# Experts' weights streamed in pairs of panels, 16 KB per partition in one row

## The chip, the cores and the metric

One core of a Trainium2 chip runs the whole program. The metric is the device time of one execution in microseconds, as the median of the runs; smaller is better.

## What is computed

Three transformer blocks follow each other on 256 tokens of width 1024, all in f32. The change touches only the experts' layer of the second block: every token picks 4 of 32 experts, and each expert is a two-layer network of its own.

```python
N_EXPERTS = 32; TOP_K = 4; D_FF_EXPERT = D_MODEL   # 1024
logits = xt @ router_w + router_b
top_logit, top_idx = lax.top_k(logits, TOP_K)
top_gate = jax.nn.softmax(top_logit, axis=-1)
...
# for every expert e, on the tokens that picked it:
#   hidden = x_e @ w1[e] + b1[e]        w1[e]: 1024 x 2048, 8 MB
#   glu, lin = the two halves of hidden, clipped to 7
#   act = glu * sigmoid(1.702 * glu) * (lin + 1)
#   y_e = act @ w2[e] + b2[e]           w2[e]: 1024 x 1024, 4 MB
# the output sums gate * y_e over the four experts of a token
```

## The kernel before

The first and the third block and the second block's mixers read their weights through `core.ring`, six places (`RING`) of 8 KB per partition (`SLOT`, 2048 f32), 1 MB each. The experts' layer takes those six places over and adds a tensor of its own, `expert_ring`, which has eleven more.

An expert's weights are twelve panels of 1 MB. Panels 0 to 7 are rows of `w1`: the array `w1` is laid out so that panel j is 128 rows of 8 KB, one for each partition. Panels 8 to 11 are `w2`, two blocks of 128 rows of 4 KB each, which go side by side into a place. Of the 17 places, twelve hold one panel number each; the other five are second places for panels 0 to 4 (`TWICE`), used by experts of odd number, so that these panels of the next expert can be on their way while the present ones are still in use.

The work goes in units, a unit being one expert with at most 64 of its tokens. Here there are 32 units. TensorE does, in this order for each unit u: the bias (L2733), panels 0 to 7 (L2738, eight matmul instructions a panel), the scatter of the unit before (L2514), the gather of the next unit's tokens (L2486), turns of gates, hidden values and tokens (L2747, L2752, L2492), a bias (L2757), and panels 8 to 11 (L2768). Ahead of each panel it waits for that panel's own semaphore (`panel(j)`), and behind each it counts up `used`. VectorE and ScalarE do the activation (L2797 to L2803, L2780) in the time of scatter and gather.

SyncE (SP) issues all loads, in an order that is written out: the function `load` waits until `used` tells that the place is free and issues one transfer of 1 MB. Up to `AHEAD` (units 0 to 17) panels 0 to 4 of unit u+1 are issued ahead of panels 5 to 11 of unit u; from there on, behind them. Unit 0 and the second places are filled by `load_first`, during the end of the mixers (L2862, L2864). When the last unit is done, its scatter and the residual add follow, the block ends, and the third block's first loads are issued (L246).

Of the kernel before, what the change touches and what calls it, by code (L numbers as in the profile page):

```python
# [6 lines left out]
F32 = mybir.dt.float32  # L7
# [7 lines left out]
P = 128  # L15
TOK = 256
NB = TOK // P
D = 1024
# [4 lines left out]
RING = 6  # L23
SLOT = KG * PANEL
# [13 lines left out]
N_EXPERTS, TOP_K = 32, 4  # L38
# [101 lines left out]
class Signal:  # L140


    def __init__(self, sem):
        self.sem, self.base, self.raised = sem, 0, 0
# [2283 lines left out]
def mixture_of_experts(core, h, norm, bias, ring, rw):  # L2428
# [6 lines left out]
    with ExitStack() as s:  # L2435
# [14 lines left out]
        used = ring.used  # L2450
# [7 lines left out]
        def pair_count(eng):  # L2458
            return eng.value_load(unit_int[0:1, MAX_UNITS:MAX_UNITS + 1], min_val=E // 2, max_val=MAX_UNITS // 2)
# [43 lines left out]
        def scatter(pe, u):  # L2503

            pe.wait_ge(copied.sem, copied.at(u))
            pe.wait_ge(gates_copied.sem, gates_copied.at(u))

            pe.wait_ge(added.sem, added.at(u * 4))  # L2510
            for t in range(4):
                for i, (rows, _) in enumerate(halves):

                    mm = pe.matmul(ps[:, 2 + 2 * i + t // 2, t % 2 * TOK:t % 2 * TOK + TOK], ytok[rows, t * P:t * P + P],  # L2514
                                   selt[rows, :], start=True, stop=True)
                    if t % 2 == 1:
                        mm.then_inc(scattered.sem, 1)
# [8 lines left out]
        with ExitStack() as s2:  # L2526
# [14 lines left out]
            with core.block() as block:  # L2541
                @block.gpsimd
                def _(pool):
                    pool.memset(acc[:, :, :], 0.0)

                    pool.memset(ytok[:, :], 0.0)
                    pool.memset(selt[:, :], 0.0).then_inc(cleared.sem, 1)
# [138 lines left out]
        with core.block() as block:  # L2686
            @block.sync
            def _(sp):
                def load(u, turn, panels, odd, e):
                    for j in panels:  # L2690

                        sp.wait_ge(used.sem, turn * PANELS + (j + 1))
                        sp.dma_start(ring.panel(j, odd), ring.weights(e, j)).then_inc(ring.loaded_at(j, odd).sem, 16)

                def expert(u):
                    return sp.value_load(unit_int[0:1, bass.ds(u, 1)], min_val=0, max_val=E - 1)
                twice, once = range(TWICE), range(TWICE, PANELS)

                with sp.Fori(1, AHEAD) as v:
                    load(v * 2, v * 2 - 2, twice, 0, v * 2)  # L2700
                    load(v * 2 - 1, v * 2 - 2, once, 1, v * 2 - 1)
                    load(v * 2 + 1, v * 2 - 1, twice, 1, v * 2 + 1)
                    load(v * 2, v * 2 - 1, once, 0, v * 2)

                def in_turn(v, before, even, odd):
                    load(v * 2 - 1, v * 2 - 2, once, 1, before)
                    load(v * 2, v * 2 - 2, twice, 0, even)
                    load(v * 2, v * 2 - 1, once, 0, even)
                    load(v * 2 + 1, v * 2 - 1, twice, 1, odd)
                with sp.Fori(AHEAD, E // 2 - 1) as v:  # L2710
                    in_turn(v, v * 2 - 1, v * 2, v * 2 + 1)
                n = pair_count(sp)
                with sp.Fori(E // 2 - 1, n) as v:
                    in_turn(v, expert(v * 2 - 1), expert(v * 2), expert(v * 2 + 1))
                last = sp.value_load(unit_int[0:1, MAX_UNITS + 1:MAX_UNITS + 2], min_val=E // 2 - 1, max_val=MAX_UNITS // 2 - 1)
                load(last * 2 + 1, last * 2, once, 1, expert(last * 2 + 1))

            @block.tensor
            def _(pe):
                n = pair_count(pe)  # L2720
                with pe.Fori(0, n) as v:
                    for odd in range(2):
                        u = v * 2 + odd
                        def panel(j):
                            sig = ring.loaded_at(j, odd)
                            pe.wait_ge(sig.sem, sig.at((v if j < TWICE else u) * 16 + 16))
                            return ring.flat(j, odd)
                        pe.wait_ge(expert_picked.sem, expert_picked.at(u + 1))
                        pe.wait_ge(xg_ready.sem, xg_ready.at(u + 1))

# [31 lines left out]
                        for q in range(4):  # L2762
                            w = panel(8 + q)
                            for i in range(2):
                                k = 2 * q + i
# [53 lines left out]
                                             in1=core.x[:, k, :], op0=ALU.mult, op1=ALU.add)  # L2819


PANELS, TWICE, AHEAD = 12, 5, 9


class ExpertRing:


    def __init__(self, core, s):
        self.core = core
        self.more = s.enter_context(core.nc.sbuf_tensor("expert_ring", [P, PANELS - RING + TWICE, SLOT], F32))  # L2830
        self.loaded = [core.counter(f"expert_panel{j}") for j in range(PANELS + TWICE)]
        self.used = core.counter("expert_panel_used")

    def slot(self, j, odd):

        return PANELS + j if odd and j < TWICE else j

    def loaded_at(self, j, odd):
        return self.loaded[self.slot(j, odd)]

    def flat(self, j, odd=0):
        n = self.slot(j, odd)
        return self.core.ring[:, n, :] if n < RING else self.more[:, n - RING, :]

    def panel(self, j, odd=0):
        return self.flat(j, odd) if j < 8 else self.flat(j, odd).rearrange("p (k n) -> p k n", n=D)

    def weights(self, e, j):

        if j < 8:  # L2850
            return self.core.a["w1"][bass.ds(e * 8 + j, 1)].rearrange("a p n -> p (a n)")
        return self.core.a["w2"][bass.ds(e * 4 + (j - 8), 1)].rearrange("a (k p) n -> p (a k) n", p=P)

    def load_first(self, sp):

        core = self.core
        total = len(core.stream)
        for j in [*range(RING, PANELS), *range(RING)]:
            if j < RING:

                sp.wait_ge(core.panel_used.sem, core.panel_used.at(range(j, total, RING)[-1] + 1))
            sp.dma_start(self.panel(j), self.weights(0, j)).then_inc(self.loaded[j].sem, 16)  # L2862
        for j in range(TWICE):
            sp.dma_start(self.panel(j, 1), self.weights(1, j)).then_inc(self.loaded_at(j, 1).sem, 16)  # L2864


def moe_layer(core, h, bias, ring, rw):
# [491 lines left out]
def tokens_last(x):  # L3359

    return np.ascontiguousarray(x.reshape(x.shape[0], -1, P).transpose(2, 1, 0))
# [35 lines left out]
def layout(i):  # L3397
    f = {k: np.asarray(v) for k, v in i.items()}
    a = {"x": tokens_last(f["x"][0]), "p": np.stack([tokens_last(f["p"][l, 0]) for l in range(DEPTH)])}
# [6 lines left out]
    for l in range(DEPTH):  # L3406
        g, u = f["w_ffn_gate"][l].reshape(D, FF_T, P), f["w_ffn_up"][l].reshape(D, FF_T, P)
# [34 lines left out]
    a["lora"] = np.ascontiguousarray(np.concatenate([  # L3442
        np.concatenate([f["decay_up_2"][0], f["iclr_up_2"][0]], axis=0), f["gate_up_2"][0]], axis=1))
    a["router"] = np.ascontiguousarray(f["router_w_2"][0].reshape(DT, P, N_EXPERTS).transpose(1, 0, 2))
    a["w1"] = f["exp_w1_2"][0].reshape(N_EXPERTS * 8, P, SLOT)
    a["w2"] = f["exp_w2_2"][0].reshape(N_EXPERTS * 4, 2 * P, D)
    a["eb"] = np.ascontiguousarray(np.concatenate([f["exp_b1_2"][0], f["exp_b2_2"][0]], axis=1))

    w = f["w_in_3"][0]
# [29 lines left out]
```

## Time and profile before

| | us |
|---|---|
| median of 3 runs | 2482.25 |
| lowest, highest | 2480.29, 4030.77 |
| the profiled execution's own time | 2479.19 |
| its span, first to last instruction | 2477.4 |
| TensorE busy | 2321.4 (94%) |
| DMA, bytes moved | 619.06 MB, mean 250 GB/s |

The profiled execution is 3.06 us below the median, and 1.8 us of its own time lie outside the span. The span is cut into 40 slices of about 62 us in the page's rows of digits; the experts' layer is the long stretch from slice 21 to slice 36. The mean over the span hides that the core's DMA engines are busy to a quite different degree in that stretch than elsewhere.

### The profile page before, as it was taken

The page shows a single profiled execution, that of the slowest core. Times are in us where ns is not written, and L with a number is a line of the kernel's source. Part 1 is how long each engine was busy: PE and PEld are TensorE (multiplying, and loading weights), DVE is VectorE, ACT ScalarE, POOL GpSimd, SP SyncE. Part 2 cuts the span into 40 slices and gives each one's busy share as a digit, 9 for nine tenths or more (in the row PEclk, how much of TensorE's full clock was granted, in tenths as well). Part 3 has the DMA queues.
Part 4 walks back from the last instruction along what each step waited for, and adds up shares of the span by engine and source line. Part 5 has one row for each costly group of instructions (what it writes and reads, how often), then busy time and mean ns, then how long its engine had stood idle before and what let it go on. Part 6 is the DMA issues. An engine that isn't in the chain of part 4 may idle for free. (4 is left out here: it accounts for less than half of the span.)

```text
span 2477.4 us, 31797 instructions
## 1 busy us (share of the span) xinstructions
PE 2321.4 (94%) x12991; PEld 1532.0 (62%) x12991; DVE 660.2 (27%) x1448; ACT 395.8 (16%) x824; POOL 71.1 (3%) x80
## 2 busy tenths in 40 slices
PE   8999999999899999998789999999999999979998
PEld 7778788877688877876633333333333333348786
DVE  3142100024300022626223222222222222242222
ACT  2210110014200012224201000000110000012331
POOL 0110010000000000011000000000000000000000
PEclk9999999999999999999889999999999999989999
DMA  6334644455754454310669999999999999952422
GB/s 262 119 104 145 214 153 144 159 195 190 296 188 153 140 190 139 134 36 2 283 265 417 417 418 417 417 417 418 416 417 417 418 417 417 417 225 94 162 71 91
DMA packets 105020, 619.06 MB, mean 250 GB/s; under 512 B 9856, under 2 KB 11136, under 8 KB 48128
## 3 DMA queue, kind: packets, MB, share of 16 engines
q1 hardware_dynamic: 103216, 611.10, 63.3%
q10 hardware_dynamic: 1712, 6.63, 0.8%
q8 instruction: 71, 1.16, 0.2%
q14 instruction: 21, 0.17, 0.0%
HBM read 616.63 MB, written 1.05 MB: 249 GB/s over the span
## 5 line engine op out<-in xcount | busy, mean ns | idle before, releaser
L391 PE MATMUL ps<-x_res,ring 128*128 128x256 f32 x2560 | 568.6, 383 | 21.3 <-ACT x_res L953 12.9
L391 PEld LDWEIGHTS ps<-x_res,ring 128*128 128x128 f32 x2560 | 488.5, 192 | 97.5 <-issue 22.4
L2738 PE MATMUL ps<-expert_ring,moe_xg 128*64 128x512 f32 x1152 | 262.4, 596 | 24.4 <-DMA expert_ring<-w_dram 24.3
L391 PE MATMUL ps<-first_arena,ring 128*128 128x256 f32 x1088 | 239.4, 379 | 1.4 <-DMA ring<-w_o_dram 1.4
L2768 PE MATMUL ps<-expert_ring,mix_y 128*64 128x512 f32 x1024 | 226.8, 595 | 0.0
L391 PEld LDWEIGHTS ps<-first_arena,ring 128*128 128x128 f32 x1088 | 206.6, 190 | 29.8 <-DMA ring<-w_o_dram 1.8
L2738 PE MATMUL ps<-ring,moe_xg 128*64 128x512 f32 x896 | 202.8, 598 | 15.8 <-DMA ring<-w_dram 15.2
L2738 PEld LDWEIGHTS ps<-expert_ring,moe_xg 128*64 128x64 f32 x1152 | 78.1, 136 | 197.7 <-issue 126.1
L391 PE MATMUL ps<-third_h,ring 128*128 128x256 f32 x768 | 176.2, 386 | 5.1 <-ACT third_h L274 3.9
L391 PEld LDWEIGHTS ps<-third_h,ring 128*128 128x128 f32 x768 | 147.5, 194 | 28.1 <-issue 6.5
L2768 PEld LDWEIGHTS ps<-expert_ring,mix_y 128*64 128x64 f32 x1024 | 70.6, 137 | 133.4 <-issue 133.4
L2738 PEld LDWEIGHTS ps<-ring,moe_xg 128*64 128x64 f32 x896 | 62.4, 137 | 146.4 <-issue 103.8
L2797 DVE TENSOR_SCALAR mix_y<-ps 128x512 f32<-128x512 f32 x32 | 22.1, 691 | 473.2 <-PE ps L2738 473.2
L2780 ACT ACTIVATE mix_y<-mix_y 128x512 f32<-128x512 f32 x32 | 20.2, 630 | 713.7 <-DVE mix_y L2797 713.7
L391 PE MATMUL ps<-mix_arena,ring 128*128 128x256 f32 x416 | 95.5, 387 | 4.3 <-ACT mix_arena L274 4.3
L1413 DVE TENSOR_TENSOR first_arena<-first_arena,ps 128x256 f32<-128x256 f32 x44 | 18.5, 421 | 288.4 <-PE ps L391 288.4
L391 PEld LDWEIGHTS ps<-mix_arena,ring 128*128 128x128 f32 x416 | 79.1, 193 | 17.3 <-issue 6.1
L2523 DVE TENSOR_TENSOR moe_acc<-moe_acc,ps 128x512 f32<-128x512 f32 x132 | 81.5, 680 | 1.3 <-PE ps L2514 1.3
L2812 DVE COPY moe_ytok<-ps 128x512 f32<-128x512 f32 x32 | 22.1, 692 | 176.1 <-PE ps L2768 176.1
L2514 PEld LDWEIGHTS ps<-moe_selt,moe_ytok 64*128 64x128 f32 x528 | 48.3, 186 | 32.1 <-issue 27.7
L2486 PE MATMUL ps<-moe_ht,moe_sel 128*64 128x512 f32 x264 | 65.7, 619 | 1.6 <-DVE moe_sel L2465 1.6
L2514 PE MATMUL ps<-moe_selt,moe_ytok 64*128 64x256 f32 x528 | 65.9, 389 | 0.9 <-DVE moe_ytok L2812 0.9
(529 smaller groups left out, 1939.2 us busy)
## 6 DMA issues: line engine op xcount, KB each, us to landing
expert_ring<-w_dram SPq DMA_DIRECT2D x272, 1024.0 KB, 22.4
ring<-w_dram SPq DMA_DIRECT2D x112, 1024.0 KB, 19.3
ring<-w_in_dram SPq DMA_DIRECT2D x55, 1024.0 KB, 4.9
ring<-ffn_up_dram SPq DMA_DIRECT2D x44, 1024.0 KB, 4.8
ring<-ada_dram SPq DMA_DIRECT2D x36, 1024.0 KB, 5.0
ring<-w_out_dram SPq DMA_DIRECT2D x16, 1024.0 KB, 5.0
ring<-ffn_dn_dram SPq DMA_DIRECT2D x16, 1024.0 KB, 5.0
ring<-ple_g_dram SPq DMA_DIRECT2D x8, 1024.0 KB, 7.0
```

The lines of the kernel that those rows point to most:

```text
L391: mm = pe.matmul(core.ps[:, t % BANKS, 0:TOK], w[:, k * PANEL + c * P:k * PANEL + c * P + P], sources[panel](k0 + k), start=(k0 + k == 0), ...
L1413: return e.tensor_tensor(h[:, j, :], h[:, j, :], ps, ALU.mult)
L2486: mm = pe.matmul(ps[out, 6, :], sel[:, b, :], ht[:, b, at:at + 512], start=(b == 0), stop=(b == NB - 1))
L2514: mm = pe.matmul(ps[:, 2 + 2 * i + t // 2, t % 2 * TOK:t % 2 * TOK + TOK], ytok[rows, t * P:t * P + P], selt[rows, :], start=True, stop=True)
L2523: dve.tensor_tensor(part, part, ps[:, 2 + 2 * i + q, :].rearrange("p (k n) -> p k n", n=TOK), ALU.add).then_inc(added.sem, 1)
L2738: mm = pe.matmul(ps[out, bank, :], xg[:, j % 4, j // 4, :], w[:, bank * D + at:bank * D + at + 512], start=False, stop=(j == 7))
L2768: mm = pe.matmul(ps[out, 2, :], hidt[:, at_k:at_k + S], w[:, i * D + at:i * D + at + 512], start=False, stop=(k == DT - 1))
L2780: act.activation(sg[:, :], glu[:, :], ACT.Sigmoid, scale=SWIGLU_ALPHA).then_inc(sig_ready.sem, 1)
L2797: dve.tensor_scalar(glu[:, :], ps[:, 0, :], SWIGLU_LIMIT, None, ALU.min).then_inc(glu_ready.sem, 1)
L2812: dve.tensor_copy(ytok[:, :], ps[:, 2, :]).then_inc(copied.sem, 1)
```

## The change

The weights of the experts are laid out anew, outside the timed program: one array `we` holds six pairs of panels for each expert, and a pair is 128 rows of 16 KB, contiguous in memory, panel 2q in the first half of each row and panel 2q+1 in the second. That goes for w2 too, whose rows were 4 KB. One transfer brings a pair, 2 MB, and counts up one semaphore. There are eight places for pairs, 16 KB per partition each: three in `core.ring`, five in `expert_ring`. Six hold one pair number each, two are second places for pairs 0 and 1, that is for panels 0 to 3. TensorE waits at every second panel, for the pair; SP waits until both panels of a pair are used. The order in which SP issues, by units, is kept.

```diff
--- before.py
+++ after.py
@@ -2686,15 +2686,15 @@
         with core.block() as block:
             @block.sync
             def _(sp):
-                def load(u, turn, panels, odd, e):
-                    for j in panels:
-
-                        sp.wait_ge(used.sem, turn * PANELS + (j + 1))
-                        sp.dma_start(ring.panel(j, odd), ring.weights(e, j)).then_inc(ring.loaded_at(j, odd).sem, 16)
+                def load(u, turn, pairs, odd, e):
+                    for q in pairs:
+
+                        sp.wait_ge(used.sem, turn * PANELS + (2 * q + 2))
+                        sp.dma_start(ring.pair(q, odd), ring.weights(e, q)).then_inc(ring.loaded_at(q, odd).sem, 16)
 
                 def expert(u):
                     return sp.value_load(unit_int[0:1, bass.ds(u, 1)], min_val=0, max_val=E - 1)
-                twice, once = range(TWICE), range(TWICE, PANELS)
+                twice, once = range(TWICE), range(TWICE, PAIRS)
 
                 with sp.Fori(1, AHEAD) as v:
                     load(v * 2, v * 2 - 2, twice, 0, v * 2)
@@ -2722,9 +2722,10 @@
                     for odd in range(2):
                         u = v * 2 + odd
                         def panel(j):
-                            sig = ring.loaded_at(j, odd)
-                            pe.wait_ge(sig.sem, sig.at((v if j < TWICE else u) * 16 + 16))
-                            return ring.flat(j, odd)
+                            if j % 2 == 0:
+                                sig = ring.loaded_at(j // 2, odd)
+                                pe.wait_ge(sig.sem, sig.at((v if j // 2 < TWICE else u) * 16 + 16))
+                            return ring.panel(j, odd)
                         pe.wait_ge(expert_picked.sem, expert_picked.at(u + 1))
                         pe.wait_ge(xg_ready.sem, xg_ready.at(u + 1))
 
@@ -2819,7 +2820,7 @@
                                              in1=core.x[:, k, :], op0=ALU.mult, op1=ALU.add)
 
 
-PANELS, TWICE, AHEAD = 12, 5, 9
+PANELS, PAIRS, TWICE, AHEAD = 12, 6, 2, 9
 
 
 class ExpertRing:
@@ -2827,41 +2828,42 @@
 
     def __init__(self, core, s):
         self.core = core
-        self.more = s.enter_context(core.nc.sbuf_tensor("expert_ring", [P, PANELS - RING + TWICE, SLOT], F32))
-        self.loaded = [core.counter(f"expert_panel{j}") for j in range(PANELS + TWICE)]
+        self.fixed = RING // 2
+        self.more = s.enter_context(core.nc.sbuf_tensor("expert_ring", [P, PAIRS - self.fixed + TWICE, 2 * SLOT], F32))
+        self.loaded = [core.counter(f"expert_pair{q}") for q in range(PAIRS + TWICE)]
         self.used = core.counter("expert_panel_used")
 
-    def slot(self, j, odd):
-
-        return PANELS + j if odd and j < TWICE else j
-
-    def loaded_at(self, j, odd):
-        return self.loaded[self.slot(j, odd)]
-
-    def flat(self, j, odd=0):
-        n = self.slot(j, odd)
-        return self.core.ring[:, n, :] if n < RING else self.more[:, n - RING, :]
+    def slot(self, q, odd):
+
+        return PAIRS + q if odd and q < TWICE else q
+
+    def loaded_at(self, q, odd):
+        return self.loaded[self.slot(q, odd)]
+
+    def pair(self, q, odd=0):
+        n = self.slot(q, odd)
+        if n >= self.fixed:
+            return self.more[:, n - self.fixed, :]
+        return self.core.ring[:, 2 * n:2 * n + 2, :].rearrange("p a n -> p (a n)")
 
     def panel(self, j, odd=0):
-        return self.flat(j, odd) if j < 8 else self.flat(j, odd).rearrange("p (k n) -> p k n", n=D)
-
-    def weights(self, e, j):
-
-        if j < 8:
-            return self.core.a["w1"][bass.ds(e * 8 + j, 1)].rearrange("a p n -> p (a n)")
-        return self.core.a["w2"][bass.ds(e * 4 + (j - 8), 1)].rearrange("a (k p) n -> p (a k) n", p=P)
+        return self.pair(j // 2, odd)[:, j % 2 * SLOT:j % 2 * SLOT + SLOT]
+
+    def weights(self, e, q):
+        return self.core.a["we"][bass.ds(e * PAIRS + q, 1)].rearrange("a p n -> p (a n)")
 
     def load_first(self, sp):
 
         core = self.core
         total = len(core.stream)
-        for j in [*range(RING, PANELS), *range(RING)]:
-            if j < RING:
-
-                sp.wait_ge(core.panel_used.sem, core.panel_used.at(range(j, total, RING)[-1] + 1))
-            sp.dma_start(self.panel(j), self.weights(0, j)).then_inc(self.loaded[j].sem, 16)
-        for j in range(TWICE):
-            sp.dma_start(self.panel(j, 1), self.weights(1, j)).then_inc(self.loaded_at(j, 1).sem, 16)
+        for q in [*range(self.fixed, PAIRS), *range(self.fixed)]:
+            if q < self.fixed:
+
+                both = max(range(j, total, RING)[-1] for j in (2 * q, 2 * q + 1))
+                sp.wait_ge(core.panel_used.sem, core.panel_used.at(both + 1))
+            sp.dma_start(self.pair(q), self.weights(0, q)).then_inc(self.loaded[q].sem, 16)
+        for q in range(TWICE):
+            sp.dma_start(self.pair(q, 1), self.weights(1, q)).then_inc(self.loaded_at(q, 1).sem, 16)
 
 
 def moe_layer(core, h, bias, ring, rw):
@@ -3442,8 +3444,10 @@
     a["lora"] = np.ascontiguousarray(np.concatenate([
         np.concatenate([f["decay_up_2"][0], f["iclr_up_2"][0]], axis=0), f["gate_up_2"][0]], axis=1))
     a["router"] = np.ascontiguousarray(f["router_w_2"][0].reshape(DT, P, N_EXPERTS).transpose(1, 0, 2))
-    a["w1"] = f["exp_w1_2"][0].reshape(N_EXPERTS * 8, P, SLOT)
-    a["w2"] = f["exp_w2_2"][0].reshape(N_EXPERTS * 4, 2 * P, D)
+    a["we"] = np.concatenate([
+        f["exp_w1_2"][0].reshape(N_EXPERTS, 4, 2, P, SLOT).transpose(0, 1, 3, 2, 4).reshape(N_EXPERTS, 4, P, 2 * SLOT),
+        f["exp_w2_2"][0].reshape(N_EXPERTS, 2, 4, P, D).transpose(0, 1, 3, 2, 4).reshape(N_EXPERTS, 2, P, 2 * SLOT),
+    ], axis=1).reshape(N_EXPERTS * PAIRS, P, 2 * SLOT)
     a["eb"] = np.ascontiguousarray(np.concatenate([f["exp_b1_2"][0], f["exp_b2_2"][0]], axis=1))
 
     w = f["w_in_3"][0]
```

## Rows read from the trace of the kernel before

**Rows 1.** The page: 40 slices of the span, and the DMA queues.

```profile
PEclk9999999999999999999889999999999999989999
DMA  6334644455754454310669999999999999952422
GB/s 262 119 104 145 214 153 144 159 195 190 296 188 153 140 190 139 134 36 2 283 265 417 417 418 417 417 417 418 416 417 417 418 417 417 417 225 94 162 71 91
...
q1 hardware_dynamic: 103216, 611.10, 63.3%
```

**Rows 2.** Windows of the experts' layer: busy per engine, TensorE's clock, DMA share, GB/s.

```profile
1500.00:1700.00 200.00, 184.42 (x910) 65.53 (x904) 49.46 (x115) 20.18 (x30) 0.00 (x0) 1.00 1.02 418
1900.00:2100.00 200.00, 184.57 (x906) 65.03 (x906) 50.95 (x115) 20.80 (x31) 0.00 (x0) 1.00 1.02 417
```

**Rows 3.** Windows inside one unit: first w1 panels on the way, then w2.

```profile
1537.00:1554.00 17.00, 15.51 (x76) 4.95 (x74) 1.18 (x4) 0.00 (x0) 0.00 (x0) 1.00 1.01 421
1526.50:1534.50 8.00, 7.52 (x46) 3.58 (x44) 5.72 (x11) 2.79 (x5) 0.00 (x0) 1.00 1.03 412
```

**Rows 4.** Timeline of TensorE, a unit of the long stretch: start, us, operation [idle before].

```profile
1525.27 1.94 PE L2738 MATMUL ps<-expert_ring,moe_xg 128*64 128x512 f32 x8 [0.56 <-DMA expert_ring<-w_dram]
1527.14 2.00 PE L2514 MATMUL ps<-moe_selt,moe_ytok 64*128 64x256 f32 x16
...
1533.41 7.09 PE L2768 MATMUL ps<-expert_ring,mix_y 128*64 128x512 f32 x32
...
1540.76 8.75 PE L2738 MATMUL ps<-ring,moe_xg 128*64 128x512 f32 x40
1550.46 1.94 PE L2738 MATMUL ps<-ring,moe_xg 128*64 128x512 f32 x8 [0.95 <-DMA ring<-w_dram]
1552.94 1.94 PE L2738 MATMUL ps<-expert_ring,moe_xg 128*64 128x512 f32 x8 [0.55 <-DMA expert_ring<-w_dram]
1555.43 1.94 PE L2738 MATMUL ps<-expert_ring,moe_xg 128*64 128x512 f32 x8 [0.55 <-DMA expert_ring<-w_dram]
```

**Rows 5.** Timeline of TensorE, units 0 and 1.

```profile
1256.09 11.74 PE L2738 MATMUL ps<-ring,moe_xg 128*64 128x512 f32 x48
...
1277.46 7.09 PE L2768 MATMUL ps<-expert_ring,mix_y 128*64 128x512 f32 x32
...
1284.82 8.75 PE L2738 MATMUL ps<-expert_ring,moe_xg 128*64 128x512 f32 x40
1293.40 1.89 PE L2738 MATMUL ps<-ring,moe_xg 128*64 128x512 f32 x8
...
1304.92 5.37 PE L2768 MATMUL ps<-expert_ring,mix_y 128*64 128x512 f32 x24
```

**Rows 6.** Line L2693, the issues of the long stretch: ns min/median/max, first and last start; landing.

```profile
L2693 SPq DMA_DIRECT2D expert_ring<-w_dram x261: 332/384/7590, 1269.7 to 2163.5; - x131
...
L2693 SPq DMA_DIRECT2D ring<-w_dram x106: 332/876/9690, 1259.4 to 2150.7; - x106
...
DMA to landing us min/median/max: 4.7/21.4/26.2
```

**Rows 7.** DMA issues in narrow windows at 1259.4, 1288.6, 2163.5: KB, us to landing.

```profile
ring<-w_dram SPq DMA_DIRECT2D x1, 1024.0 KB, 4.7
...
expert_ring<-w_dram SPq DMA_DIRECT2D x1, 1024.0 KB, 10.6
...
expert_ring<-w_dram SPq DMA_DIRECT2D x1, 1024.0 KB, 23.4
```

**Rows 8.** Windows at the start of the program, with rows of 8 KB and of 13.3 KB.

```profile
10.00:15.00 5.00, 5.00 (x18) 3.59 (x17) 0.00 (x0) 0.43 (x1) 0.00 (x0) 1.00 1.02 422
15.00:20.00 5.00, 5.00 (x24) 3.07 (x22) 1.87 (x4) 1.24 (x2) 0.00 (x0) 1.00 1.01 424
```

**Rows 9.** Timeline, the last unit and the start of the third block.

```profile
2176.69 1.94 PE L2738 MATMUL ps<-expert_ring,moe_xg 128*64 128x512 f32 x8 [0.58 <-DMA expert_ring<-w_dram]
...
2184.83 7.09 PE L2768 MATMUL ps<-expert_ring,mix_y 128*64 128x512 f32 x32
...
2200.05 4.92 SPq L246 DMA_DIRECT2D ring<-w_in_dram  x6
```

## The prediction, made before the changed kernel was run

> **What bounds the kernel now.** I read the page's slices first, to find out whether the changed stage has a limit of its own. TensorE is busy nearly everywhere, so the total says little. But from slice 21 to slice 34 the DMA digits are 9, the rate is 415 to 418 GB/s in nearly every slice, and TensorE's clock is at full speed [rows 1]. The windows say it in numbers: DMA share 1.02 and 417 to 418 GB/s over 200 us each, TensorE busy for 184 of 200 us [rows 2]. The stage moves 32 experts of 12.58 MB through a stream that never pauses. 12.58 MB at 417.5 GB/s are 30.14 us, and TensorE's timeline repeats after 1555.43 - 1525.27 = 30.16 us [rows 4]. In each such unit TensorE waits three times, always for the DMA of a panel, 0.95 + 0.55 + 0.55 = 2.05 us [rows 4]. Where it doesn't wait, in units 0 and 1, a unit takes 1304.92 - 1277.46 = 27.46 us, and a panel 8.58 / 5 = 1.716 us [rows 5]. So the DMA stream is the bound, TensorE could be 2.7 us (9%) faster in each unit, and the change is worth what it does to the stream's rate. SP doesn't matter: a load is issued 21.4 us (median) ahead of its landing [rows 6].
>
> **The price of a row.** The trace has two row lengths in one stream. In rows of 8 KB (w1) panels come every 1552.94 - 1550.46 = 2.48 and 2.49 us [rows 4], four in a row at the end of the stage as well, and I take 2.49. Eight of them leave 30.16 - 19.92 = 10.24 us for the four panels of w2, 2.56 us each, in rows of 4 KB. The windows inside a unit give the same two rates, 421 against 412 GB/s [rows 3], so 2.49 and 2.55 us. Each of 16 DMA engines carries 8 rows of 8 KB for a panel of w1 and 16 rows of 4 KB for one of w2; 0.07 us for 8 rows are 8.75 ns a row, on top of the bytes. That is the estimate on which the sum rests: rows of 16 KB mean 4 rows an engine for each MB.
> - w1: 4 rows fewer a MB, 2.49 - 0.035 = 2.455 us.
> - w2: 12 rows fewer, 2.56 - 0.105 = 2.455 us.
> - A pair 4.91 us; a unit of six pairs 29.46 us against 30.16, that is 0.70 us (2.3%) less.
>
> No row shows 16 KB. Bounds: if nothing is gained beyond 8 KB, a pair takes 4.98 us and only w2 gains, 29.88 a unit. If the whole cost of rows goes, the bytes alone take 2.49 - 8 x 0.00875 = 2.42 us a MB, 4.84 a pair, 29.04 a unit. I take the value between them, because the nearest row supports it: the first stage mixes rows of 8 KB with a transfer of 13.3 KB rows at 422 to 424 GB/s [rows 8], a bit above the 421 of 8 KB alone. 4.91 us a pair are 427 GB/s. Against the change there is the other end: long rows may hold something up, and the farthest row in that direction is that of w2, 2.56 us a MB or 5.12 a pair.
>
> Against this stands a rule of the Trainium skill, DMA: Bandwidth & Descriptors, "Why small descriptors are slow (HBM only)": each packet costs about 3 cycles and each descriptor 32 bytes besides, and putting descriptors together pays only up to 256 bytes. An estimate by that page (3 cycles of 850 MHz and 32 bytes at 27 GB/s) is 4.7 ns a row, a pair would take 4.94 us, and the sum below would be -12 us. The trace has nearly twice that price between 4 and 8 KB. The same page's table ("Measured") has 341 GB/s at 1 MB with a fixed 2 us for each DMA, by which bigger transfers would gain much; this trace disagrees, with 421 GB/s at 1 MB back to back, so I count nothing for the size of a transfer.
>
> **What pairs cost, step by step.**
> - One wait on TensorE in place of two, half as many issues on SP: off the path. An issue takes 0.33 us when nothing is in its way; the 9.69 us of the longest [rows 6] is time in which much is already queued.
> - TensorE gets panel 6 only when panel 7 is there too. In the long stretch, with time 0 at the landing of pair 3 (panels 6, 7): panel 7 starts 1.72 us later than now, w2 at 8.14 + 1.72 = 9.86, the next unit's panel 0 at 9.86 + 7.35 = 17.2 [rows 4], panel 2 at 20.6, panel 4 at 24.1. Pairs land at 4.9, 9.8 (w2), 14.7, 19.6, 24.55, 29.46. So pairs 4, 5, 0 and 1 are there in time, pair 2 is waited for by 0.5 us, pair 3 by 1.5. The period stays that of the stream. Granularity costs once, in the last unit.
> - Places come free later (both panels used), and there are 16 instead of 17. Does the stream run dry? The worst case is pair 4: it is used at 9.86 + 3.43 = 13.3, so the next one can be issued then, 2.2 us ahead of its bytes (4.7 for a lone transfer less its 2.49 [rows 7]). Its turn in the stream comes at 29.46, behind the two pairs of w2 and pairs 0 to 3. That leaves 14 us. Pair 2 is used at -1.5 (landed -4.9, used +3.43) and has its turn at 19.6. No gap.
> - At the start, all of unit 0 lies in place before TensorE begins, now as then. Before: the first issue is at 1259.4; at 1288.6 + 10.6 = 1299.2 31 panels have landed [rows 6, 7]: 17 at first, and 14 after. After: pair 4 of unit 1 waits for panel 9, used at 1277.46 + 3.43 = 1280.9 plus some 0.4 [rows 5], and lands 2.2 + 4.91 us later at 1288.4; pair 5 at 1293.3; the next at 1298.2. Then 30 panels have landed, since one was missing at the start. Remaining: 354 panels, 177 pairs.
> - 177 x 4.91 = 869.1, so the last pair lands at 2167.3, and pair 3 of the last unit 9.8 us earlier, at 2157.5. Panel 7 starts at 2159.2, against 2176.69 [rows 9]. Behind that point nothing changes: 8.14 us to w2, then the end of the stage and the third block's first load at 2200.05. (Before, the same reckoning holds: the last panel lands at 2163.5 + 23.4 = 2186.9 [rows 6, 7], 353 panels in 887.7 us, 2.515 each, which is 30.18 a unit.)
>
> Sum: 2159.2 - 2176.7 = -17.5 us. In parts: the stream -18.6 (887.7 against 869.1), its start -1.0, the last unit +2.1 (1.7 for panel 7 behind 6, 0.4 because w2 ends sooner behind pair 3). Against the profiled execution, 2479.19 - 17.5 = 2461.7; against the median, 2482.25 - 17.5 = 2464.7. Two of the three runs stand at 2480 and 2482, so the median is the upper of two like runs, and I say 2464, or 0.7% less. The other stages are untouched.
>
> **The rivals.**
> - *Long rows bring nothing more (the change doesn't do what it says).* 8 KB is long enough, or the chip cuts 16 KB in two. A pair takes 4.98, the sum is 177 x 0.07 = 12.4 us worse: -5 us, 2477. For it: two row lengths only are in the stream. Against it: the rate in the first stage [rows 8]. (The Trainium skill's rule of DMA: Bandwidth & Descriptors, above, ends between this rival and the forecast, at the edge of the forecast's own spread; the step between 4 and 8 KB speaks against it.)
> - *The rest of the cost goes too*, with half the completion writes, which I counted in the row's price: a pair at 4.84, -30 us, 2452. TensorE would still not be the bound: 27.46 + two restarts is below 29.04.
> - *Slower: rows of 16 KB stream worse*, because each engine reads or writes one place for twice as long. It decides from 4.91 + 17.5 / 177 = 5.01 us a pair, 419 GB/s. At w2's rate of today, 5.12, it is +20 us, 2502; over 2% slower would take 5.29 (396 GB/s). Nothing in the rows points to it, and the first stage speaks against it [rows 8].
> - *Slower: the coarser ring runs dry.* Were the 14 us of reserve wrong by all of it, every unit would have a gap of 2.2 us or more, 29 x 2.2 = +64 us, 2529. It decides when the release of pair 4 comes after 27.3 on the clock above; now 13.3.
>
> **How the numbers follow.** Forecast 0.66 (with sizes from -10 to -25 around it), nothing more from long rows 0.15, all of the cost gone 0.10, long rows worse 0.07, ring dry 0.02. The range from 2450 to 2481 takes in the bounds 4.84 and 4.98 (2452 and 2477), with 2 to 4 us for the spread of the runs, and leaves out both slower cases. 2% are 50 us, about what a measurement of this kernel can tell from no change; to be faster by that a pair would have to take 4.73 us, at 444 GB/s. So faster 0.01, within 2% 0.95, slower 0.04 (ring dry, and the far end of worse rows).
>
> **What would show it.** The page's packets should fall from 105,020 by the halving of w1's and the quartering of w2's. In the slices of the stage 417 should become 427 GB/s; 421 throughout would be the first rival. TensorE should wait twice in a unit, some 0.5 and 1.5 us, at panels 4 and 6, with a period of 29.46 us and no difference between w1 and w2. A rate under 417 in windows of a unit with DMA share near 1 is worse rows; a share under 1 is the ring. I should be wrong above all if the 8.75 ns is not a cost per row but something of w2's layout (two rows of memory into one place).

## The result, and the profile after

The changed kernel takes 2452.38 us (median of 4 runs, 2449.48 to 2455.07), against 2481.27 for the kernel before. One of the four runs before stood at 4030.77 us; without it the median is 2480.29, the ratio 0.9887, with a 95% interval of 0.9875 to 0.9899, and the difference 27.9 us or 1.1%. The forecast was 2464, range 2450 to 2481.

The page of the kernel after, with the rows that answer to [rows 1]:

```profile
PEclk9999999999999999999889999999999999989999
DMA  6323644445754444310579999999999999942422
GB/s 265 120 103 138 225 154 146 146 180 187 291 218 154 142 154 176 132 59 2 208 290 429 427 428 429 428 429 428 428 428 428 428 428 428 428 193 90 172 69 86
DMA packets 60986, 619.03 MB, mean 252 GB/s; under 512 B 6784, under 2 KB 8064, under 8 KB 12288
...
q1 hardware_dynamic: 59184, 611.08, 62.3%
```

The same bytes go in 60,986 packets instead of 105,020. The slices of the experts' layer stand at 427 to 429 GB/s where they stood at 416 to 418. The windows of the long stretch say the same as numbers (busy of PE, PEld, DVE, ACT, POOL; TensorE's clock; DMA share; GB/s), beside [rows 2]:

```profile
1500.00:1700.00 200.00, 186.11 (x928) 67.65 (x926) 51.11 (x115) 20.63 (x31) 0.00 (x0) 1.00 1.01 428
1900.00:2100.00 200.00, 186.08 (x925) 67.31 (x922) 49.24 (x112) 19.60 (x29) 0.00 (x0) 1.00 1.01 428
```

TensorE's timeline in that stretch, to be held against [rows 4]; the idle time ahead of a row and what ended it stand in brackets:

```profile
1508.33 3.65 PE L2739 MATMUL ps<-ring,moe_xg 128*64 128x512 f32 x16 [0.25 <-DMA ring<-we_dram]
1513.22 3.65 PE L2739 MATMUL ps<-expert_ring,moe_xg 128*64 128x512 f32 x16 [1.24 <-DMA expert_ring<-we_dram]
1516.80 2.00 PE L2514 MATMUL ps<-moe_selt,moe_ytok 64*128 64x256 f32 x16
...
1523.07 7.09 PE L2769 MATMUL ps<-expert_ring,mix_y 128*64 128x512 f32 x32
...
1530.42 7.04 PE L2739 MATMUL ps<-ring,moe_xg 128*64 128x512 f32 x32
1537.73 3.65 PE L2739 MATMUL ps<-ring,moe_xg 128*64 128x512 f32 x16 [0.27 <-DMA ring<-we_dram]
1542.62 3.65 PE L2739 MATMUL ps<-expert_ring,moe_xg 128*64 128x512 f32 x16 [1.24 <-DMA expert_ring<-we_dram]
```

The period is 1537.73 - 1508.33 = 29.40 us (forecast 29.46), a pair 1513.22 - 1508.33 = 4.89 (forecast 4.91). Two waits are left in a unit, for pairs 2 and 3, 0.27 and 1.24 us (forecast 0.5 and 1.5).

So far the forecast holds. But the whole gain in this trace is larger, and the timelines show where it is. First the kernel before, around the end of the mixers' last block (all engines; SPq is SyncE's issues):

```profile
1202.43 8.66 SPq L2862 DMA_DIRECT2D ring<-w_dram  x6
...
1209.34 0.88 DVE L2391 SCALAR_TENSOR_TENSOR x_res<-ps,modulations,x_res 128x256 f32<-128x256 f32 x2 [2.58 <-PE ps L2357]
1211.13 5.75 SPq L2864 DMA_DIRECT2D expert_ring<-w_dram  x5
1217.35 1.80 POOL L2544 MEMSET moe_acc<- 128x2048 f32 x1 [42.39 <-POOLq L2374]
```

and the kernel after, with its first panel in unit 0 and the third block's first load as last rows:

```profile
1209.30 0.88 DVE L2391 SCALAR_TENSOR_TENSOR x_res<-ps,modulations,x_res 128x256 f32<-128x256 f32 x2 [2.58 <-PE ps L2357]
1210.13 0.91 SPq L2866 DMA_DIRECT2D expert_ring<-we_dram  x2
1211.52 1.80 POOL L2544 MEMSET moe_acc<- 128x2048 f32 x1 [36.51 <-POOLq L2374]
...
1248.36 9.97 PE L2739 MATMUL ps<-ring,moe_xg 128*64 128x512 f32 x38
...
2160.11 7.09 PE L2769 MATMUL ps<-expert_ring,mix_y 128*64 128x512 f32 x32
...
2175.34 3.07 SPq L246 DMA_DIRECT2D ring<-w_in_dram  x6
```

In both, VectorE ends the block's arithmetic at 1210.2. The routing (its first row is the memset on POOL) begins when the last engine leaves the block. Before, that was SP: its five issues of L2864 end at 1211.13 + 5.75 = 1216.88, and the routing begins at 1217.35. After, SP is done at 1211.04, and the routing begins at 1211.52, 5.8 us earlier. The windows show TensorE around it. Kernel before:

```profile
1209.00:1217.00 8.00, 0.30 (x2) 0.00 (x0) 0.88 (x2) 0.00 (x0) 0.00 (x0) 0.83 1.03 419
1217.00:1224.00 7.00, 5.26 (x16) 4.05 (x16) 0.59 (x2) 2.97 (x10) 2.52 (x3) 0.71 1.02 419
```

Kernel after:

```profile
1211.50:1218.00 6.50, 3.72 (x16) 2.96 (x16) 1.83 (x3) 3.07 (x10) 2.52 (x3) 1.00 1.01 426
```

Before, TensorE does nothing for 8.6 us, its granted clock falls to 1.2 GHz for part of both windows (0.83 and 0.71 on the mean), and the sixteen matmuls of the norm take 5.26 us. After, the gap is 2.8 us, the clock stays at 2.4 GHz and they take 3.72. That is another 1.5 us in these two traces. It is not shown that the shorter gap gave it: in a second profiled execution of the same kernel (after_again, below) the gap is just as short, and the clock fell all the same (first the row of TensorE's timeline, then a window).

```profile
1213.74 5.41 PE L517 MATMUL ps<-mix_y,mat 128*128 128x256 f32 x16 [2.85 <-ACT mix_y L524]
1213.10:1219.60 6.50, 5.41 (x16) 4.10 (x16) 0.58 (x2) 2.65 (x9) 2.52 (x3) 0.74 1.01 429
```

Of the thirteen traces of the table below, the clock was low at this place in all five with a gap of 6.3 us or more, and in two of the eight with a gap of 1.9 to 3.0 us.

The sum over the trace: the first panel of unit 0 starts at 1248.36 instead of 1256.09 [rows 5], 7.7 us earlier; from there to the third block's first load it takes 926.98 us instead of 2200.05 - 1256.09 = 943.96 [rows 5, 9], 17.0 us less. Together 24.7 us at that load; at the end of the span it is 24.2. The medians differ by 27.9. The profiled execution of the kernel after was the slowest of its four, and later runs of the same kernel, below, had a median of 2455.6, 24 us under that of the kernel before on the same chip. So the trace accounts for 24 to 25 us, and the rest is spread between executions.

The experiments ran on three chips; each ratio is to the kernel before on the same chip, where its medians were 2481.7 (before_late, pairs_8k, pairs_4k and pairs_halves), 2480.4 (w2_8k, pairs_evens, after_late, three_second) and 2479.2 us (after_again, three_smooth, triples). In the table below, each kernel's stage is cut in the same way: A is from the first load of experts' weights to the first panel's matmul of unit 0, B from there to the third block's first load. All times are read from the timelines of the profiled executions.

| kernel | A, us | B, us | GB/s, 1500 to 1700 | median, us | ratio to before, 95% |
|---|---|---|---|---|---|
| before | 60.9 | 944.0 | 418 | 2480.3 | |
| after | 53.2 | 927.0 | 428 | 2452.4 | 0.9875 to 0.9899 |
| before_late | 55.9 | 944.5 | 418 | 2472.6 | 0.9953 to 0.9978 |
| w2_8k | 62.3 | 937.1 | 421 | 2472.3 | 0.9960 to 0.9984 |
| pairs_8k | 53.5 | 941.3 | 421 | 2470.2 | 0.9940 to 0.9975 |
| pairs_4k | 60.6 | 966.4 | 410 | 2499.2 | 1.0049 to 1.0088 |
| pairs_halves | 60.3 | 1855.3 | 212 | 3387.2 | 1.3603 to 1.3679 |
| pairs_evens | 60.4 | 927.7 | 428 | 2462.8 | 0.9908 to 0.9943 |
| after_late | 53.3 | 926.9 | 428 | 2454.9 | 0.9883 to 0.9911 |
| after_again | 55.9 | 927.0 | 428 | 2455.6 | 0.9887 to 0.9917 |
| three_second | 53.3 | 924.2 | 428 | 2454.2 | 0.9881 to 0.9910 |
| three_smooth | 53.3 | 922.1 | 428 | 2449.4 | 0.9861 to 0.9891 |
| triples | 53.8 | 929.7 | 430 | 2460.5 | 0.9907 to 0.9934 |

### The profile page after: what moved, and what is told of

It reads as the page before. It is cut to its first block and busy times, and to the rows that moved or that the text cites. A ratio compares the mean times of both kernels' runs of the same rounds, so it can differ in the third digit from the quotient of the medians.

```text
span 2453.2 us, 31056 instructions
## 1 busy us (share of the span) xinstructions
PE 2313.1 (94%) x12991; PEld 1534.8 (63%) x12991; DVE 660.4 (27%) x1448; ACT 395.5 (16%) x824; POOL 71.1 (3%) x80
## 2 busy tenths in 40 slices
DMA packets 60986, 619.03 MB, mean 252 GB/s; under 512 B 6784, under 2 KB 8064, under 8 KB 12288
## 3 DMA queue, kind: packets, MB, share of 16 engines
q1 hardware_dynamic: 59184, 611.08, 62.3%
## 5 line engine op out<-in xcount | busy, mean ns | idle before, releaser
L2739 PE MATMUL ps<-expert_ring,moe_xg 128*64 128x512 f32 x1024 | 228.9, 594 | 24.8 <-DMA expert_ring<-we_dram 24.8
L2739 PE MATMUL ps<-ring,moe_xg 128*64 128x512 f32 x1024 | 229.5, 598 | 5.2 <-DMA ring<-we_dram 5.2
L2739 PEld LDWEIGHTS ps<-expert_ring,moe_xg 128*64 128x64 f32 x1024 | 71.3, 137 | 171.3 <-issue 124.8
L2739 PEld LDWEIGHTS ps<-ring,moe_xg 128*64 128x64 f32 x1024 | 72.3, 138 | 152.7 <-issue 127.2
L1413 DVE TENSOR_TENSOR first_arena<-first_arena,ps 128x256 f32<-128x256 f32 x44 | 18.6, 422 | 288.3 <-PE ps L391 288.3
```

What stands on the lines that cost most here:

```text
L1413: return e.tensor_tensor(h[:, j, :], h[:, j, :], ps, ALU.mult)
L2739: mm = pe.matmul(ps[out, bank, :], xg[:, j % 4, j // 4, :], w[:, bank * D + at:bank * D + at + 512], start=False, stop=(j == 7))
```

## The experiments

Two questions were open: whether it is the length of the rows that made the stream faster, or the size and number of the transfers; and whether SP really held the routing back.

**before_late: the start.** The kernel before, with one edit: the loop over the second places leaves `load_first`, in the mixers' last block, and SP runs it in the routing block (the first hunk).

```diff
+                @block.sync
+                def _(sp):
+                    ring.load_second(sp)
...
+
+    def load_second(self, sp):
         for j in range(TWICE):
             sp.dma_start(self.panel(j, 1), self.weights(1, j)).then_inc(self.loaded_at(j, 1).sem, 16)
```

> The kernel before, with one edit: the five loads of unit 1's second places are issued by SP in the routing block instead of at the end of the mixers' last block. Theory A (SP held the block's end: its last issue took 3.86 us because much was queued, the routing began at 1217.4 instead of 1211.5, and TensorE's clock fell in the gap): routing begins near 1211.5, w2 of unit 0 near 1270 instead of 1277.5, everything later by the same 7 us earlier, 2474 us. Rival B (the earlier start came from the smaller or coarser ring itself, 16 places and six first transfers): routing begins at 1217.4 as before, 2481 us. In both the stream stays at 417 GB/s and 30.16 us a unit.

Measured: 2472.6 us, B unchanged. Its timeline (all engines):

```profile
1210.70 6.88 SPq L2870 DMA_DIRECT2D expert_ring<-w_dram  x5
1210.70 1.81 POOL L2544 MEMSET moe_acc<- 128x2048 f32 x1 [35.25 <-POOLq L2374]
```

SP's five issues take even longer, 6.88 us, but the routing now begins with them, 16.35 us behind the first load instead of 22.14. Theory A on the start holds, rival B falls: nothing of the ring was changed here, and the routing starts 5.8 us earlier, as in the kernel after. A gained 5.0 us rather than 7; in this execution TensorE's clock was low at the routing's start too (0.76 on the mean from 1211 to 1218), though it had been without work for only 2.8 us. The medians differ by 9.1 us, the two profiled executions by 5.6: the trace accounts for the smaller figure.

**pairs_8k and pairs_4k: the rows.** The changed kernel; only the layout of `we` and the shape of the copy differ (4 in place of 2 for pairs_4k).

```diff
-        return self.core.a["we"][bass.ds(e * PAIRS + q, 1)].rearrange("a p n -> p (a n)")
+        return self.core.a["we"][bass.ds((e * PAIRS + q) * 2, 2)].rearrange("a p n -> p a n")
...
-                        sp.dma_start(ring.pair(q, odd), ring.weights(e, q)).then_inc(...)
+                        sp.dma_start(ring.pair(q, odd).rearrange("p (a n) -> p a n", a=2), ring.weights(e, q)).then_inc(...)
```

> The changed kernel (pairs, transfers of 2 MB, the same ring, waits and order), but the array is laid out so that each pair comes in 256 rows of 8 KB, two for each partition. Theory A (a price of 8.75 ns for each row on each DMA engine): a pair takes 4.98 us, 421 GB/s, a unit 29.88 us; 177 pairs x 0.08 = +14 us against the changed kernel, and up to 6 us more if SP is held at the end of the mixers again: 2466 to 2472 us. Rival C (the size or number of the transfers made the gain): a pair 4.90 us, 428 GB/s, 2452 us.

> The same with 512 rows of 4 KB for each pair, four for each partition. Theory A: a pair takes 5.12 us, 410 GB/s, a unit 30.72 us; 177 x 0.22 = +39 us against the changed kernel, plus 6 to 10 us for SP held at the end of the mixers: 2497 to 2501 us, slower than the kernel before. Rival C: 2452 us. If the 2.56 us of w2's panels came from something else than the length of rows (two blocks of memory put into one place), the rate would lie at 421 as with 8 KB.

Measured: 2470.2 and 2499.2 us, both inside what theory A gave. Windows of pairs_8k:

```profile
1500.00:1700.00 200.00, 183.31 (x906) 65.67 (x904) 45.86 (x106) 18.38 (x27) 0.00 (x0) 1.00 1.01 421
```

and of pairs_4k:

```profile
1500.00:1700.00 200.00, 178.21 (x890) 65.05 (x888) 50.95 (x115) 20.80 (x31) 0.00 (x0) 1.00 1.02 410
```

Transfers of 2 MB run at 421 GB/s in rows of 8 KB and at 410 in rows of 4 KB, the rates of w1 (421) and w2 (2.56 us a panel, which is 410) in the kernel before [rows 3, 4]. Rival C falls: the size of the transfer gives nothing. The two also show SP. pairs_8k isn't held at the start (A 53.5), though some of its issues in the long stretch take up to 3.7 us. pairs_4k is held at the start again (A 60.6), and in the long stretch its issues into `ring` read, by line L2693 (ns min/median/max),

```profile
L2693 SPq DMA_DIRECT2D ring<-we_dram x61: 372/4672/9734, 1263.1 to 2171.7; - x61
```

where the kernel after has

```profile
L2693 SPq DMA_DIRECT2D ring<-we_dram x61: 332/333/356, 1253.8 to 2119.8; - x61
```

The records of single rows in the traces show their price too. On an engine a row of 4, 8, 16 and 24 KB takes 164, 313, 614 and 915 ns (medians from 1400 to 2000 us in pairs_4k, pairs_8k, after and triples, the last being the kernel with 24 KB rows below). From 8 KB on, 8 KB more cost 301 ns each time, so some 12 ns of each row are not bytes; the write of 4 bytes that reports a completion takes 9.

**w2_8k: w2's rows alone.**

```diff
-        return self.core.a["w2"][bass.ds(e * 4 + (j - 8), 1)].rearrange("a (k p) n -> p (a k) n", p=P)
+        return self.core.a["w2"][bass.ds(e * 4 + (j - 8), 1)].rearrange("a p n -> p (a n)")
```

> The kernel before with one part of the change alone: w2 is laid out so that its panels, too, are 128 rows of 8 KB. Single panels, 17 places, transfers of 1 MB, waits and order as before. Theory A (price of a row): all panels at 2.49 us, a unit 29.88 us instead of 30.16, 421 GB/s; 29.4 units x 0.28 = -8 us. If w2's shorter rows at the end of the mixers are also what keeps SP from its last issue, 6 to 7 us more go, and the result is 2466 to 2467; if not, 2473. Rival C (size of transfers): no change of the rate, 417 GB/s, 2481.

Measured: 2472.3 us, at 421 GB/s. B is 6.9 us shorter (theory A: 8). A is not: SP was held as before,

```profile
1210.16 5.43 SPq L2864 DMA_DIRECT2D expert_ring<-w_dram  x5
1216.06 1.80 POOL L2544 MEMSET moe_acc<- 128x2048 f32 x1 [40.58 <-POOLq L2374]
```

so w2's short rows were not what held it (A is even 1.4 us longer than before: the routing starts 0.3 us sooner but takes 1.7 longer, with TensorE's clock low at its start as before). With this run the change falls into three steps, on B: w2 in rows of 8 KB -6.9 us; single panels to pairs at equal rows (w2_8k to pairs_8k) +4.2; rows of 8 to rows of 16 KB (pairs_8k to after) -14.3. The sum is -17.0, as measured.

**pairs_halves and pairs_evens: the size of the transfer at rows of 16 KB.** Each pair in two transfers of 1 MB, and TensorE waits for both. For pairs_halves:

```diff
-                        sp.dma_start(ring.pair(q, odd), ring.weights(e, q)).then_inc(ring.loaded_at(q, odd).sem, 16)
+                        for low in (0, P // 2):
+                            sp.dma_start(ring.pair(q, odd)[low:low + P // 2], ring.weights(e, q)[low:low + P // 2]).then_inc(
+                                ring.loaded_at(q, odd).sem, 16)
```

For pairs_evens the slices are `[low:P:2]`, with low 0 and 1.

> The changed kernel with rows of 16 KB, but each pair in two transfers of 1 MB, partitions 0 to 63 and 64 to 127. Theory A (only the rows count): a pair 4.90 to 4.92 us, 428 GB/s, 2452 us within 3. Rival C (the transfer's size counts): at 1 MB a transfer the rate is 421 GB/s or less, 2466 us. If 64 partitions at a time use the DMA engines less evenly, the rate falls well below 417, which says nothing on either.

> The changed kernel with rows of 16 KB, each pair in two transfers of 1 MB, this time the even and the odd partitions. Theory A (only the rows count): 428 GB/s, 2452 us within 3. Rival C (2 MB in one transfer is part of the gain): 421 GB/s or less, 2466 or more. The run with partitions 0 to 63 and 64 to 127 had 212 GB/s: if that came from half of the partitions as such, this one has 212 as well; if from which partitions, it has not.

Measured: 3387.2 us for the halves. Its windows:

```profile
1500.00:1700.00 200.00, 120.32 (x490) 40.52 (x488) 29.51 (x67) 12.25 (x18) 0.00 (x0) 0.78 1.01 212
```

The DMA share is 1.01, so the engines were never idle, at half the rate of the kernel after; TensorE waits long enough for its clock to fall (0.78). With even and odd partitions, again 64 at a time, the rate is 428 GB/s:

```profile
1500.00:1700.00 200.00, 187.15 (x932) 67.98 (x930) 51.73 (x119) 20.80 (x31) 0.00 (x0) 1.00 1.01 428
```

So rows of 16 KB have their rate at 1 MB a transfer too, and rival C falls from this side as well. The total of pairs_evens, 2462.8, is still 11 us above what I expected; B is right (927.7), and A is 7.2 us too long. SP's issues behind the last release of a place are eight instead of four, at 0.6 us each; they end at 1216.51 + 2.51 = 1219.02, 19.1 us behind the first load (1199.95), where the kernel after has 15.9. That is 3.2 us; the rest, 4 us, is nearly all in the routing itself, with TensorE's clock low at its start (0.51 on the mean from 1219.5 to 1226):

```profile
1216.51 2.51 SPq L2870 DMA_DIRECT2D expert_ring<-we_dram  x4
```

Here nothing holds SP; it is only slower to get through, and the block waits for it all the same.

**after_late: the control.** The edit of before_late in the kernel after.

> The changed kernel with the loads of the second places issued in the routing block. Control for theory A on the start: in the changed kernel SP isn't held, its last issue ends at 1211.0 and VectorE's last add at 1210.2, so at most 0.5 to 1 us is to be had: 2451 to 2452 us. If it gains 6 us as in the kernel before, the theory is wrong.

Measured: 2454.9 us, an interval that covers the one of the kernel after. The routing begins at 1210.94, with the first load at 1195.53: 15.4 us behind it instead of 16.4, so 1.0 us was to be had at that point, and nothing of it is left at the first panel (A 53.3).

**three_second, three_smooth, after_again: further.** Both versions have nine places for pairs and issue the second places in the routing block. Core of the edit; three_smooth has the last part as well.

```diff
-PANELS, PAIRS, TWICE, AHEAD = 12, 6, 2, 9
+PANELS, PAIRS, TWICE, AHEAD = 12, 6, 3, 9
...
-        xt, xg = sb("xt", [P, D // 2]), sb("xg", [P, 4, 2, S])
+        xg = sb("xg", [P, 4, 2, S])
+        xt = sg
...
+                flat = acc[0:shape[0], :, :].rearrange("p k n -> p (k n)")[:, taken[0]:taken[0] + n]
...
-                with sp.Fori(AHEAD, E // 2 - 1) as v:
+                at = AHEAD * 2
+                load(at - 1, at - 2, [3], 1, at - 1)
+                load(at, at - 2, [0], 0, at)
+                load(at - 1, at - 2, [4, 5], 1, at - 1)
+                load(at, at - 2, [1, 2], 0, at)
+                load(at, at - 1, once, 0, at)
+                load(at + 1, at - 1, twice, 1, at + 1)
+                with sp.Fori(AHEAD + 1, E // 2 - 1) as v:
```

> A version beyond the change: a third second place (pair 2), 9 places of pairs, with the second places issued in the routing block. Room for it comes from laying the routing's small tensors over the accumulator, which is cleared afterwards, and the gathered tokens over the sigmoid's tile. With theory A the stream has one pair less to bring after the start of the units: -4.9 us, and with 0.5 to 1 us of the earlier start 2446 to 2447 us; period 29.4 us as before. Rival: the period is set by TensorE and pair granularity in part, then it gets shorter than 29.4 and the gain is larger; or the new wait of ScalarE for the hidden values costs some 0.1 us a unit in units 0 to 9 and nothing after.

Measured: 2454.2 us, 7 us above what I expected and hardly under after_late on the same chip (2454.9); B is 924.2, 2.7 of the expected 4.9 us. Two windows find the rest of B:

```profile
1720.00:1740.00 20.00, 17.86 (x94) 7.17 (x96) 7.45 (x17) 2.42 (x4) 0.00 (x0) 1.00 0.89 361
1740.00:1760.00 20.00, 19.52 (x102) 7.58 (x100) 5.66 (x11) 2.73 (x5) 0.00 (x0) 1.00 1.01 430
```

The stream stood still once (DMA share 0.89 in 20 us, so some 2 us), where SP passes from its first order to its second.

> The version with a third second place, and the order of SP's issues mended at unit 17, where it changes from one order to the other and the stream of the first version stood still once for 2 us: pair 0 of unit 18 goes ahead of pairs 4 and 5 of unit 17. Theory A: no gap in the stream after unit 1, from the first panel to the third block 922.5 us against 927.4 in the changed kernel, 2447 to 2448 us if the stages before cost the same. Rival: what is gained at the start is lost again in the order or in the stages before, and it stays at 2452 to 2454.

> The changed kernel itself once more, on the chip of the next two, as their measure: 2452 us within 3, a unit 29.4 us, the routing at 16.4 us behind the first load.

Measured on one chip: three_smooth 2449.4 us, the kernel after 2455.6, the kernel before 2479.2. That is 1.4 us above what I had given for three_smooth, and 0.6 us above for the kernel after. B is 922.1 us against 927.0: the 4.9 us of one pair, as expected (the expectation counted B from the weight load ahead of the first matmul, 0.4 us earlier). The ratios' intervals, 0.9861 to 0.9891 and 0.9887 to 0.9917, just overlap, so by the totals three_smooth is probably faster than the kernel after; that its stage is 4.9 us shorter is shown by the trace.

after_again also shows how far executions of one kernel differ: A is 55.9 us here and 53.2 in the first trace of the same program, with B equal to 0.1 us. The routing starts 16.35 us behind the first load in both; the 2.7 us lie behind that point, 1.7 of them in the sixteen matmuls that ran with the clock low.

**triples: longer rows still.** Three panels in a row of 24 KB, four triples a unit, five places.

```diff
-PANELS, PAIRS, TWICE, AHEAD = 12, 6, 2, 9
+PANELS, PAIRS, TWICE, AHEAD = 12, 4, 1, 9
...
-                        sp.wait_ge(used.sem, turn * PANELS + (2 * q + 2))
+                        sp.wait_ge(used.sem, turn * PANELS + (3 * q + 3))
```

> Rows of 24 KB: triples of panels, transfers of 3 MB, four triples a unit and one second place, 15 panels in all instead of 16. Theory A: a MB costs 2.42 + 2.67 x 0.00875 = 2.443 us, a triple 7.33, 429 GB/s, a unit 29.3; 0.1 us a unit is gained (-2.4 us), and one panel less in place (+2.5), the first release later (+1.7) and the last unit's w1 in a triple with w2's first panel (+2.5 to 4) cost more: 2456 to 2458 us. Rival (the coarser ring runs dry, as in the prediction's last rival): a gap in the stream in every unit, DMA share under 1, over 2470.

Measured: 2460.5 us, against 2455.6 for the kernel after on the same chip.

```profile
1500.00:1700.00 200.00, 186.19 (x932) 68.39 (x932) 48.95 (x115) 19.61 (x29) 0.00 (x0) 1.00 1.00 430
```

The rate rises once more, to 430 GB/s, the DMA share stays at 1.00, and yet B is 2.7 us longer. By the landings in the trace, the last triple is there 911.9 us behind the first panel's matmul, the last pair of the kernel after 911.6, so the start has used up what the rate gave; and from there to the third block's first load it takes 17.8 us instead of 15.3. The total is 2.5 us above the range that I gave. The rival, a gap in each unit, did not occur.

## Why the prediction was right, and where it was not

- *The bound.* Right (though the lowest of the stage's slices before is 416 GB/s, not 415). With the stream 2.5% faster in rate, B became 1.8% shorter, and TensorE still waits twice a unit.
- *The price of a row.* Right, and now a line of four points. From 410, 421, 428 and 430 GB/s a panel (1.0486 million bytes) takes 2.56, 2.49, 2.45 and 2.44 us in rows of 4, 8, 16 and 24 KB, that is with 16, 8, 4 and 2.67 rows for each engine. The first step gives 0.07 / 8 = 8.8 ns a row, the second 0.04 / 4 = 10; the third is within the rounding of the rates. Single rows show 12 ns, a bit more than the stream's rate does. The forecast took 8.75 from the first step alone. The first rival (nothing beyond 8 KB) would need 421, and the second (all of it gone) 433.
- *The rule against it.* The Trainium skill, DMA: Bandwidth & Descriptors, "Why small descriptors are slow (HBM only)", has 3 cycles a packet and 32 bytes a descriptor, 4.7 ns by the estimate in the prediction; the runs have about twice that, and between 8 and 16 KB it was worth 14.3 us here. Its table of sizes, which the prediction holds against the trace, is for transfers that GpSimd issued; here SP issued them, so the 421 GB/s don't contradict it.
- *What pairs cost.* Right in kind and close in size. At equal rows it is +4.2 us (w2_8k to pairs_8k); the terms of the forecast (one panel less in place 2.45, start -1.0, last unit 2.1) make 3.55. In the long stretch no gap appeared, with the reserve of 14 us, nor with triples.
- *The sum for the part that the forecast covered*: -17.5 forecast, -17.0 measured. That it is so close is partly luck, since two terms were off in opposite directions. By the landings in the traces, the stream from the 15th pair to the last took 867.3 us against 887.6 before: -20.3, where -18.6 was forecast. But the 15th pair landed 44.3 us behind the first panel's matmul, where the forecast had 1298.2 - 1256.09 = 42.1 and the kernel before has 43.2: the start cost 1.2 us and did not give 1.0. The step there was the landing of unit 1's pair 4, put at 2.2 + 4.91 = 7.1 us behind its issue; it took 8.9, and a pair alone in the stream takes 8.2. The last unit cost 2.1, as forecast.

```profile
expert_ring<-we_dram SPq DMA_DIRECT2D x1, 2048.0 KB, 8.9
```

- *The step that failed* is the first line of "What pairs cost": "half as many issues on SP: off the path. An issue takes 0.33 us when nothing is in its way; the 9.69 us of the longest is time in which much is already queued." That is true in the long stretch, where SP is 20 us ahead, and I applied it to `load_first`, where SP's issues are the last thing in a block that all engines leave together. There SP was 6.7 us behind VectorE. The change took 5.8 us off: five issues fewer behind the last release of a place, at 0.47 us each, and 3.4 us in which the last one was held (the issues of the second places take 5.75 us before and 0.91 after, and those ahead of them end 1.0 us sooner). before_late shows these 5.8 us without any change of the ring. TensorE's clock, which did not fall in this execution, gave 1.5 us, and the rest of the routing 0.4: 7.7 us in all. These last 1.9 us can't be put down to the change, since after_again has not got them. The row was there to be read before: SP's line in the timeline ends 0.5 us ahead of the routing's first instruction.
- *The number.* 2464 was 12 us high. 5.8 us are this step, a gain by something that the forecast had put at nothing. 2 us are the base (2482 in the forecast, 2480.3 with the fourth run), and the rest lies between executions (after_again: 2455.6).

What stays open: what exactly holds an issue. I counted, for each issue of a load of experts' weights in the traces, the loads issued earlier and not yet landed, and their rows for each DMA engine:

| kernel | median when not held | median when held | not held up to |
|---|---|---|---|
| pairs_4k, 32 rows a load | 0.37 us | 4.66 us, with 4 out, 128 rows | 3 out, 96 rows |
| pairs_8k, 16 rows | 0.37 us | 3.04 us, with 6 out, 96 rows | 5 out, 80 rows |
| w2_8k, 8 rows | 0.33 us | 1.92 us, with 10 out, 80 rows | 9 out, 72 rows |
| after, 8 rows | 0.33 us | never | 6 out (the most), 48 rows |
| pairs_evens, 4 rows | 0.48 us | once, 1.3 us | 11 out, 44 rows |

In these traces, then, issues are held when many rows are out, and the longer rows of the change, half as many or fewer for the same bytes, keep the stream under that. It is not the rows alone: 80 rows in ten loads were held, 96 in three were not. No run separates the two counts further.

## What to carry to other kernels

Where a stage runs at a DMA share of 1, look for two row lengths in the trace of the stream, take the price of a row from their difference, and lay the arrays out in the longest rows that the ring's granularity allows; here rows of 4, 8, 16 and 24 KB gave 410, 421, 428 and 430 GB/s, and the last step no longer paid for its coarser ring. An engine that only issues DMAs is off the path only as long as someone else is later than it: at the end of a block, compare its last issue with the next block's first instruction, and move issues that nobody waits for across the boundary. If a transfer has to be split by partitions, even and odd ones kept the full rate here, and the two halves did not.

## What the runs showed of the hardware that I had not expected

- Transfers to partitions 0 to 63 and then 64 to 127, queued one behind the other, ran at 212 GB/s with the DMA engines busy all the time; the same bytes by even and odd partitions at 428. The Trainium skill says why, in SBUF — State Buffer, "Door 1: The DMA port swizzle": the lower 64 partitions reach only 8 of 16 ports, and bandwidth goes with the ports reached. The trace agrees: 212 is half of 428, within 1%.
- An issue on SP can be held: the issues into `ring` have a median of 4.67 us in the stream with rows of 4 KB and 0.33 us with rows of 16 KB, at nearly the same time from issue to landing (medians 23.4 and 22.0 us).
- TensorE was without work for 8.6 us, and its granted clock was 1.2 GHz for part of the next 7 us, so that sixteen matmuls took 5.26 us instead of 3.72. A gap of 2.8 us at the same place left the clock at 2.4 GHz in one execution of the kernel after; in another the gap was as long and the matmuls took 5.41 us, at 0.74 on the mean.
